# Two heads per step in the neighbourhood and the 16-head attention, with values stationary and the bias added on VectorE

## The reference

```python
# block 1: 8 heads of 64, latent queries see a window plus all context keys,
# context queries see the context keys alone (dense_attention)
s_win = einsum('bhqd,bhrqjd->bhqrj', q_r, k_w) * scale + bias
s_ctx = einsum('bhqd,bhcd->bhqc', q_r, k_ctx) * scale
p = softmax(concatenate([s_win, s_ctx]), axis=-1)
out = p_win @ v_w + p_ctx @ v_ctx
# q and k are first normalised per head: t * rsqrt(mean(t*t) + eps) * gain
# beside it a long convolution (y * x0), then
o = concatenate([attention, convolution]) @ w_out

# block 3: 16 heads of 64 (12 dilated, 4 block-sparse) over 256 tokens, causal,
# which at this length are both a masked softmax with a bias per distance
ya = rms_norm(merge_heads(oa), g_out_a)   # over 768 columns
yb = rms_norm(merge_heads(ob), g_out_b)   # over 256 columns
x = x + concatenate([ya, yb]) @ w_out
```

## Time and profile before

| | us |
|---|---|
| median of 3 runs | 2629.61 (2626.08 to 2631.86) |
| the profiled execution, whole | 2636.28 |
| its span | 2634.4 |
| PE busy | 2544.0 (97%) |
| DVE busy | 1401.5 (53%) |
| ACT busy | 1101.2 (42%) |
| POOL busy | 256.6 (10%) |

### The profile page before, as it was taken

One profiled execution on the slowest core, in us unless ns is written; L12 is line 12 of the kernel. 1 busy time (PEld: TensorE's weight loads), 2 busy tenths in 40 slices (PEclk: granted clock), 3 DMA queues, 4 the chain that ended last, 5 costly groups with the idle time before them and its releaser, 6 DMA issues.

```text
span 2634.4 us, 45491 instructions
## 1 busy us (share of the span) xinstructions
PE 2544.0 (97%) x17873; PEld 1670.0 (63%) x17873; DVE 1401.5 (53%) x2044; ACT 1101.2 (42%) x1615; POOL 256.6 (10%) x253
## 2 busy tenths in 40 slices
PE   6999999999999999999999999999999999989999
PEld 4444444455644444444444468778889898778888
DVE  7556443363465553265532444457766754556774
ACT  6434323143354442254424321345545553445553
POOL 1134001004010000100003001021100010000001
PEclk8999999999999999999999999999999999989999
DMA  9897632330056563455643243227886765324674
GB/s 302 186 183 212 172 94 80 96 96 1 17 154 185 182 190 109 122 158 181 185 136 102 74 119 97 76 85 206 237 227 176 207 191 146 113 82 127 190 210 128
DMA packets 658238, 384.21 MB, mean 146 GB/s; under 512 B 11179, under 2 KB 654608, under 8 KB 657992
## 3 DMA queue, kind: packets, MB, share of 16 engines
q1 hardware_dynamic: 653432, 369.27, 48.1%
q0 software_dynamic: 4112, 11.44, 2.8%
q10 hardware_dynamic: 576, 1.83, 0.2%
HBM read 381.41 MB, written 1.08 MB: 145 GB/s over the span
## 4 chain that ended last, share of the span: by engine, by line
PE 87%; DVE 7%; DMA 2%; ACT 2%; issue 1%; SPq 1%; POOL 0%; ACTq 0%; DVEq 0%
PE PS L659 23%; PE PS L661 23%; PE PS L660 23%; DMA arena<-in_w_mod 2%; DVE WL L1459 2%; PE PS L778 2%; PE PS L678 1%; PE PS L677 1%; PE PS L676 1%; PE PS L804 1%; PE PS L636 1%; DVE arena L1691 1%; PE PS L959 1%; PE PS L781 1%; PE PS L619 1%
## 5 line engine op out<-in xcount | busy, mean ns | idle before, releaser
L659 PE MATMUL PS<-XH,WH 128*128 128x512 f16 (+2 forms) x2912 | 946.3, 325 | 22.4 <-DVE XL L1697 14.6
L660 PE MATMUL PS<-XL,WH 128*128 128x512 f16 (+2 forms) x2912 | 945.7, 325 | 0.0
L661 PE MATMUL PS<-XH,WL 128*128 128x512 f16 (+2 forms) x2912 | 945.1, 325 | 0.0
L1043 ACT ACTIVATE WH<-W 128x1024 f16<-128x1024 f32 (+1 forms) x520 | 557.4, 1107 | 705.2 <-PE PS L661 606.3
L1459 DVE SCALAR_TENSOR_TENSOR WL<-W,WH 128x1024 f16<-128x1024 f32 (+1 forms) x520 | 669.8, 1317 | 263.3 <-ACT WH L1043 263.2
L659 PEld LDWEIGHTS PS<-XH,WH 128*128 128x128 f16 x2912 | 287.3, 99 | 206.4 <-issue 21.4
L661 PEld LDWEIGHTS PS<-XH,WL 128*128 128x128 f16 x2912 | 287.2, 99 | 181.8 <-issue 6.8
L660 PEld LDWEIGHTS PS<-XL,WH 128*128 128x128 f16 x2912 | 287.0, 99 | 171.8 <-issue 5.4
L659 PE MATMUL PS<-arena,WH 128*128 128x256 f16 (+1 forms) x1184 | 379.4, 320 | 1.3 <-DVE WL L1459 1.3
L660 PE MATMUL PS<-arena,WH 128*128 128x256 f16 (+1 forms) x1184 | 379.3, 320 | 0.0
L661 PE MATMUL PS<-arena,WL 128*128 128x256 f16 (+1 forms) x1184 | 379.2, 320 | 0.0
(11 more groups left out here) (262 smaller groups left out, 2500.0 us busy)
## 6 DMA issues: line engine op xcount, KB each, us to landing
arena<-in_w_mod SPq DMA_DIRECT2D x72, 1024.0 KB, 8.5
W<-in_ffn_a_in SPq DMA_DIRECT2D x88, 512.0 KB, 5.0
W<-in_ffn_b_in SPq DMA_DIRECT2D x88, 512.0 KB, 4.8
W<-in_w_ffn_gu SPq DMA_DIRECT2D x88, 512.0 KB, 4.3
W<-in_ret_in SPq DMA_DIRECT2D x48, 512.0 KB, 4.1
W<-in_ffn_a_out SPq DMA_DIRECT2D x32, 704.0 KB, 5.6
W<-in_ffn_b_out SPq DMA_DIRECT2D x32, 704.0 KB, 6.0
W<-in_w_ffn_down SPq DMA_DIRECT2D x32, 704.0 KB, 5.7
```

The source lines that it names most:

```text
L659: mm(dst, wh, xh, start=(kp == 0 and c == 0), stop=False, skip_group_check=True)
L660: mm(dst, wh, xl, start=False, stop=False, skip_group_check=True)
L661: return mm(dst, wl, xh, start=False, stop=(kp == g["parts"] - 1 and c == kc - 1), skip_group_check=True)
L1043: return act.activation(dst, src, ACT.Copy, scale=scale)
```

## The change

- **Pairs.** A unit of block 1 is now two neighbouring heads, whose 64 rows lie in the lower and the upper half of the partitions. Latent units: 2 heads, one tile of queries, 8 of them; context units: 2 heads, both tiles, 4 of them. Block 3 has 8 pairs, each with both tiles of queries. The two heads' scores go to banks 4+h or 4+2(u%2)+h.
- **Bias on DVE.** The flipped-identity matmul is gone. Queries are stored in reversed order within their tile (`[:, :, ::-1]`), DVE adds the bias into the score bank, and the reversal is undone when the output is read.
- **Values stationary.** Probabilities are normalised before the transposes (DVE), and the output matmul has 64 value columns stationary and 128 or 256 transposed probabilities streaming; head 0 writes partitions 0 to 63, head 1 partitions 64 to 127. The output comes out already turned, so `pe_turn_out` is gone for both.
- **Norm of block 3** by sums over partitions: a ones matmul per pair (`rel_sum`), inverse and root over 256 tokens, scaling on DVE and, for three tiles, on POOL.
- **Head factors regrouped.** The eight head-sum matmuls write four groups of 32 partitions in turn in place of one of 16. The spread and the second half of the spectrum are interleaved in two halves, and the squares stand before the last block of `even_v`.
- **Projections begin by chunk**: the first block of `even_out` and `mix_out` waits for each input chunk.

```diff
-                ins = mm(PS[0:16, 4, :], head_sum[t], qk_square[:, t, :], start=(t == 0), stop=(t == 7))
+                ins = mm(PS[32 * (t % 4):32 * (t % 4) + 32, 4, :], head_sum[t], qk_square[:, t, :], start=(t < 4), stop=(t >= 4),
+                         skip_group_check=True)
...
-            pe_attend(NA, drained(gi["even_v"]))
+            def na_score(u):
...
+                for qt in tiles:
+                    for h in range(2):
+                        rows, k0, q0 = slice(64 * h, 64 * h + 64), SEQ * part, SEQ * part + P * qt
+                        ins = mm(PS[:, 4 + 2 * (u % 2) + h, k0 * qt:k0 * qt + BOTH - k0], na_q[rows, hp, q0:q0 + P], qk1[rows, 4 + hp, k0:BOTH],
+                                 start=True, stop=True, skip_group_check=True)
+                ins.then_inc(na_scores, 1)
...
+            def na_values(u):
...
+                for i in range(BOTH // n):
+                    for h in range(2):
+                        at = 64 * (2 * hp + h)
+                        ins = mm(PS[64 * h:64 * h + 64, e % 2, P * tiles[0]:P * tiles[0] + n], V1[:, 2 * part + i, at:at + 64],
+                                 probsT[:, h, n * i:n * i + n], start=(i == 0), stop=(i == BOTH // n - 1), skip_group_check=True)
...
+            for u in range(len(NA_UNITS) + 3):
+                if u < len(NA_UNITS):
+                    na_score(u)
+                if u >= 3:
+                    na_values(u - 3)
+                if 2 <= u < len(NA_UNITS) + 2:
+                    na_turn(u - 2)
...
             pe.wait_ge(y_ready, 4)
-            pe.wait_ge(out_done, NA[1])
+            pe.wait_ge(ot_lo, 4)
...
-                pe_turn_out(O1, 4, (c,), 0)
...
-            run("even_v", between={0: copy_z, 1: qk_squares})
+            run("even_v", between={0: lambda: (copy_z(), qk_squares()), 1: lambda: None})
```

On ACT a unit is two or four exponentials and two copies of 512; on DVE (block 1):

```diff
+            def na_weigh(u):
...
+                    link(dve.reciprocal(stats[:, 2, at:at + w], stats[:, 1, at:at + w]))
+                    for j in range(w):
+                        part_p = na_p[:, 2 * (u % 2) + h, n * j:n * j + n]
+                        ins = ts(part_p, part_p, stats[:, 2, at + j:at + j + 1], None, ALU.mult)
...
+                        link(tt(PS[:, banks, 0:SEQ], PS[:, banks, 0:SEQ], na_bias[:, first:first + 3:2, :], ALU.add))
```

Block 3, on DVE and at its end on ACT:

```diff
+            for p in range(PAIRS):
+                dve.wait_ge(rel_scores, p + 1)
+                link(tt(PS[:, 4:6, 0:3 * P], PS[:, 4:6, 0:3 * P], rel_bias[:, 2 * p:2 * p + 2, :], ALU.add))
...
+                if p >= 1:
+                    kv_store(p - 1)
+                    kv_split(p + 1)
...
+            hold(PAIRS - 2)
             act.activation(warm[:, 1:2], mats[:, 1, 0:1], ACT.Sqrt)
+            root_of(0)
+            copies(PAIRS - 1)
```

More of the change, by code:

```diff
@@ L66, in shape_constants @@
                      strip[:, :P], strip[:, P:], *spread], 1)
-    head = np.arange(16)[:, None, None]
     head_spread = np.zeros((P, 8, P), f)
-    head_spread[:16] = head == 2 * np.arange(8)[:, None] + np.arange(P) // 64
+    for tile in range(8):
+        for half in range(2):
+            head_spread[32 * (tile % 4) + 14 + 2 * (tile // 4) + half, tile, 64 * half:64 * half + 64] = 1.0
     n = 2 * SEQ
@@ L414, in program @@
         UNITS = []
[L416 to L436, removed]
+        NA_UNITS = [(0, hp, (qt,)) for hp in range(4) for qt in range(2)] + [(1, hp, (0, 1)) for hp in range(4)]
+        NA_LAT = 8
         def cross_units():
@@ L678, in one @@
                                 ins = mm(dst, xl, wh, start=False, stop=(c == kc - 1))
+                    elif first and g["name"] == "mix_out":
+                        pe.wait_ge(lo_ready, 2 * w + 2)
+                        for c in range(kc):
+                            pe.wait_ge(ot_lo, 4 + c + 1)
+                            for t in range(2):
+                                ins = three(PS[:, 2 * pair + t, 0:T], t, k, kp, c)
+                    elif first and g["name"] == "even_out":
+                        pe.wait_ge(lo_ready, 2 * w + 2)
+                        pe.wait_ge(ot_lo, 4)
+                        for c in range(kc):
+                            if c >= 4:
+                                pe.wait_ge(hy_lo, c - 3)
+                            for t in range(2):
+                                ins = three(PS[:, 2 * pair + t, 0:T], t, k, kp, c)
                     elif first and g["norm"] is not None:
@@ L906, in _ @@
             pe.wait_ge(heads_back, 16)
[L907 to L911, removed]
+            for half in range(2):
+                for t in range(4 * half, 4 * half + 4):
+                    if t >= 4:
+                        pe.wait_ge(qk_ready, t - 3)
+                    mm(PS[:, 1 + t % 4, :], head_spread[:, t, :], head_root[:, :], start=True, stop=True).then_inc(qk_rstd, 1)
+                spectrum(1, range(2 * half, 2 * half + 2))
@@ new lines, in na_turn @@
+            def na_turn(u):
+                part, hp, tiles = NA_UNITS[u]
+                for h in range(2):
+                    pe.wait_ge(na_normed, 2 * u + h + 1)
+                    if u >= 1:
+                        pe.wait_ge(na_copied, 2 * (u - 1) + h + 1)
+                    for i in range(4):
+                        at = i if part == 0 else 2 * (i % 2) + i // 2
+                        ins = turn(PS[:, 2 + h, P * at:P * at + P], na_p[:, 2 * (u % 2) + h, P * i:P * i + P], eye)
+                    ins.then_inc(na_turned, 1)
@@ L1023, in _ @@
+            rel_sum(PAIRS - 1)
             pe_gemm(gi["mix_out"])
@@ L1423, in _ @@
+            kv_split(PAIRS + 1)
+            root_of(1)
+            for c in range(PAIRS_A, PAIRS):
+                act.wait_ge(rel_scaled, c - 2)
+                copy(XH[:, c, 0:SEQ], rel_o[:, c, :]).then_inc(ot_hi, 1)
             run("mix_out")
@@ L1937, in _ @@
+            group_inverse(0)
+            scaled(0)
+            scaled(1)
+            low(0)
+            scaled(2)
+            for c in range(1, 4):
+                low(c)
+            group_inverse(1)
+            low(4)
+            low(5)
+            kv_store(PAIRS - 1)
+            scaled(6)
+            scaled(7)
+            low(6)
+            low(7)
+            kv_split(PAIRS + 1)
             run("mix_out")
```

330 lines of the change are left out of this document (248 added, 82 removed).

## The result

The changed kernel takes 2557.1 us (median of four runs, 2555.3 to 2559.0) against 2630.4 for the kernel before beside it: 0.9724 of its time, interval 0.9707 to 0.9741, 73 us less. The forecast was 2568 in a range of 2556 to 2593.

The account below looks back on a forecast made before the run. PE, busy 97% of the span, was taken as the bound. Gains of 7.4 (head part), 17.6 (block 1 attention), 5.2 (behind it) and 33 (block 3) sum to 63, less 1.5: median 2629.6 to 2568, range 2556 to 2593.

Parts of the forecast that it names:

- (n+1)/2 x m: Tiled matmuls: n of length m in turn take this, one's second half overlapping the next one's first half.
- the full overlap: Upper end for tiled matmuls: half of n x m; whole kernel 2563, sharing 54% with the forecast.
- The term of the head part: Block 1 head sums: start 2.7 us sooner and take 3.9 instead of 8.54, gaining 7.4 us.
- Attention of block 1: Block 1's attention takes 53 us in place of 70.6, a gain of 17.6.
- The last pair's own way: End of block 1's attention: last pair's path from score through copy and subtraction takes 10 us.
- Behind it: After block 1's attention: four transpose groups go (1.8) and a 3.4 us piece is covered, gaining 5.2 us.
- Block 3: Block 3: pairs take 8.4 us against 11.59, first mix_out block ends at 2326, gaining 33 us.
- the 1.5 that I took off for semaphore steps: Whole kernel: added semaphore steps cost 1.5 us, subtracted from the summed gain of 63.
- DVE and ACT as the bound of block 1: Rival, block 1's attention: DVE and ACT add one microsecond per pair, 12 in all; 2580, chance 15%.
- No overlap: Rival, all tiled matmuls: tiles run one after another, gain 42.6 less 1.5; 2588.5, chance 20%.
- A price of 0.2 on every change between tiles: Rival, 184 tiled matmuls: each tile change costs like a division change; at 0.25, 2634.5, slower; chance 6%.
- The lower clock in block 1: Rival, block 1: half of 40 us of PE work runs at 1.2 GHz, adding 20; 2588, chance 5%.

Follow-up runs that it names:

- e_order: Changed kernel with one head's or tile's matmuls all issued first, then the other's, instead of in turns; 2557.55 us (0.9732 of the kernel before).
- e_same_cols: Changed kernel with both heads' outputs in the same 64 array columns instead of two halves; 2567.22 us (0.9760 of the kernel before).
- e_nopool: Changed kernel with nearly all of POOL's spectral products beside block 1's attention left out; 2551.99 us (0.9715 of the kernel before).
- the repeats: Both kernels run and profiled again unchanged; changed kernel 2556.05 us (0.9727), kernel before 2626.4 us for one execution.
- e_wait_proj: Changed kernel with the first blocks of even_out and mix_out waiting for all their input chunks again; 2563.43 us (0.9751 of the kernel before).
- e_bias_na: Changed kernel with block 1's latent bias added by identity matmuls on PE again, not by DVE; 2558.17 us (0.9734 of the kernel before).
- the fillers: Changed kernel plus five unread ones matmuls ahead of the last sum in block 3's tail; 2560.78 us (0.9737 of the kernel before).

## Why the prediction was right, and where its sizes were off

The direction and the range were right, but 2557.1 lies 1 us inside the range's lower end: I forecast 61.5 us and 73 came. Nearly every term was too small, and the largest stage came out close through errors that cancel.

- **PE's queue sets the time, so less on it is less time: right for block 3, the head sums and what stands behind the attention.** That 72 us of busy time and 73 us of time went is in part chance, since in the attention of block 1 other engines took over.
- **The overlap was mis-sized.** I took (n+1)/2 x m, half of one matmul beside half of the next. Scores cost 0.86 + 0.20, outputs 0.85 + 0.17: n/2 x m, the full overlap. What failed is the assumption that only one of a matmul's two records overlaps with its neighbour. In e_order two head sums in a row use one column group and the eight still take 1.87. The eight head sums cost 1.85, not 3.9: the four column groups run four at a time (8 x 0.86 / 4 = 1.7), and my bounds had stopped at two. Shown by e_same_cols for outputs; for scores and head sums only the lengths and starts in the trace say so. The term of the head part was 7.4 and measured 9.4 (2.7 from the start, as predicted, 6.7 from the sums). Of these 6.7, 1.6 are not overlap: at 0.86 each the eight would have taken 6.9 before, and they took 8.54, with the clock down for a part of it:

```profile
584.00:588.00 4.00, 4.00 (x7) 0.73 (x6) 0.52 (x1) 3.98 (x8) 0.00 (x0) 0.65 0.71 210
```

- **Attention of block 1: 17.6 predicted, 19.7 measured, by errors that cancel, which is luck.** A latent pair was put at 3.7, and its maxima come every 4.17 us (602.43 to 623.28 for five). Here the rival came true in which DVE and ACT become the bound. I had priced a normalisation at 0.48 and read from the earlier trace rows that POOL would not be slowed, but it is DVE that is slowed, to 1.30 (e_nopool). A context pair was put at 4.4 and takes 3.11, since an exponential of 256 with its sum costs 1.82 / 4 = 0.46, not 0.67. The last pair's own way was put at 10 and takes 11.9, from its scores, on PE's timeline,

```profile
633.38 1.14 PE L931 MATMUL PS<-arena 64*128 64x256 f32 x8
```

to the inverse transform at 645.32. From the first scores to these it takes 39.0 us where eight and three periods had made 42.8; the first two latent pairs' scores stand back to back, which I had counted as a whole period.
- **Behind it: 5.2 predicted, 4.7 measured.** The inverse transform did not wait for POOL, and the last DVE piece is covered. Some 2.4 us more were gained behind the projection's start by the clock, which I had put at nothing: 1.6 in `even_out` (44.7 us from its first matmul to the norm's sums before, 43.1 now), whose first matmuls took 0.43 before and 0.22 now, and 0.8 in a sum of that norm (1.99 before, 1.17 now). The repeats give 1.5 and 0.5. Between the head sums and the attention nothing was gained (21.6 us before, 21.5 now).
- **Block 3: 33 predicted, 34.5 measured in the first pair of profiles, 31.3 in the repeats.** I had let both sides lose the same by the clock in their thin tails; the kernel before lost some 3 us to it in one profile that it did not lose in the other. The pair takes 8.18 against 8.4, near the 8.0 of full overlap. DVE and ACT stayed under PE (34.04 and 27.10 of 45). The tail is on DVE, as predicted.
- **The start by chunk** is worth 7 us in e_wait_proj. I had named 3.4 of it for `even_out` (3.0 there), the rest is in `mix_out`.
- **Sum.** 9.4 + 19.7 + 2.4 + 4.7 + 34.5 = 70.7 against 61.5; the two profiled spans less their starts say 70.8, and the medians 73.3. The 9.2 us between 61.5 and 70.7 are 2.0 for the head sums, 2.1 for the attention, 2.4 of the clock that I had put at nothing, 1.5 in block 3 and the 1.5 that I took off for semaphore steps, less 0.5 behind the attention (rounded each).
- **Rivals.** DVE and ACT as the bound of block 1: true for the stage, at 0.5 us more per latent pair and not the 1.0 that I had priced. No overlap: refuted, outputs take 1.02 and not 1.89. A price of 0.2 on every change between tiles: refuted, sixteen records of alternating tiles take 1.02, while the 0.20 for a change of division stands (scores 0.86 + 0.20; the bias of e_bias_na 0.86 + 0.20). The lower clock in block 1: true for 5 us at 600, not for the stage. The Trainium skill, "TensorEngine Tiling (Array Packing)", Key Properties, says that changing the mode drains the array and changing the tile does not; both rows agree.
- The part of 73 us that no experiment divides is each part's share within the attention: values stationary, fewer transposes and two heads at once were not undone one by one.

## What to carry to other kernels

Two fp32 matmuls that each use half of the array's rows or columns took the time of one here, and those with a quarter of the columns a quarter of their sum; when PE is the bound, count the division changes (0.2 us each) and alternate the tiles. When that shortens a stage, list the next engine's load with its neighbours' traffic in it: here two normalisations on SBUF that cost 0.96 by their row took about 2.0 beside POOL, and moving the bias to that engine bought nothing where it was the bound and 8 us where it was not. Compare stages by a distance inside the profile when the start of the kernel varies by more than the effect, and take a second profile of both kernels: one pair alone would have put block 3 some 3 us too high, and would have given the fillers a gain that kernels without them show as well.

## What the runs showed of the hardware that I had not expected

- fp32 matmuls in different column groups overlap whole, with both of their records: the 16 records of the head sums take 1.85 us, where 0.43 each makes 6.9. PE's timeline of the changed kernel has the first four within 0.64 us, the length of one.

```profile
570.94 0.64 PE L907 MATMUL PS<-arena,mats 128*32 128x512 f32 x4
```

- The overlap hardly depends on order: two in a row per tile are free, four in a row cost 0.5 us of 1.0.
- A DVE operation between SBUF and SBUF with one source takes 0.48 us at its shortest and 1.30 beside POOL, while the bias add on PSUM (L2021) stays at 0.68 to 0.70 in the same stretch.
- A gap of 3.0 us on PE left the clock at 2.4 GHz in e_wait_proj, where the earlier trace rows shows 0.78 after a gap of 3.4. What tells the two apart was not tried.
- The same instructions can find either clock: `mix_out`'s first matmuls of the kernel before are 0.21 apart in one profile and 0.11 in the other.
- The start of the kernel differs from run to run by up to 12 us of the span, with weight transfers of 14 to 21 us on the chain in some profiles of either kernel and in none in others.
